# Prompt attention of a hybrid decoder layer: turns of two heads, the compressed branch done once, and GpSimd putting on the weights of both other branches

## The chip, the cores and the metric

The kernel runs on one core of a Trainium2 chip. It is one launch that does a whole inference step of a two-layer trunk. The metric is the device time of that launch in microseconds (us). The engines are TensorE (matmuls; PE in the profile, its weight loads are PEld), VectorE (DVE), ScalarE (ACT), GpSimd (POOL) and SyncE (SP, which issues DMAs). They run their own instruction lists and wait for each other with semaphores that are written out by hand.

## The reference

Two groups of tokens share the weights: one prompt of 256 tokens and 8 decoding sequences of 8 tokens with a past of 1024. Layer 0 mixes with recurrent heads beside twelve attention heads of 64 dimensions; three key/value heads serve four query heads each. An attention head has three branches, and only the prompt's part of it is changed here:

```python
kc = rms_norm(nsa_compress(cmp_all[:, :, 0], ...))      # one key per 32 tokens, every 16
vc = nsa_compress(cmp_all[:, :, 1], ...)
# compressed branch: softmax(q kc^T * scale + bias) vc           (16 columns for the prompt, 15 used)
# selected branch:   softmax(q ks^T * scale + bias) vs           (for 256 tokens every block is selected)
# window branch:     softmax(q kw^T * scale + bias) vw           (window 512 holds the whole prompt)
g = jax.nn.sigmoid(ng).reshape(B, T, NSA_HEADS, 3)
o_n = g[..., 0:1] * o_c + g[..., 1:2] * o_s + g[..., 2:3] * o_w
```

Every branch is causal, has its own softmax and its own gate per token and head.

## The kernel before, in words

All tiles are fp32. Layer 0 runs a feed-forward block, the projections with the recurrent heads woven in, the compress stage, prompt attention, the sample stage (the decoding sequences), an output projection, and the rest.

**Compress stage** (`pe_compress`, `act_compress`, `dve_compress`). The raw cache pages of two sequences at a time are loaded into one of two buffers `raw` (from SP's and POOL's queues, 8 pages each); the load for pair j+2 starts when the products of pair j are done. TensorE multiplies them by `w1c` in six groups g of eight matmuls (L1627). For j=0 the prompt's rows are in the same pass, so the prompt's compressed keys (columns 512 to 527 of `kc`) and values are ready after j=0. DVE adds the halves (`dve_compress_sums`, L1708 and L1712), ACT applies Silu, TensorE makes keys and values (`pe_compress_keys_values`, L1651 and L1656), ACT squares the keys, TensorE sums the squares (`pe_compress_squares`, L1665), ACT takes the root, and DVE normalizes (`dve_compress_keys`). The keys, values and squares of pair j-1 stand in TensorE's list inside the products of pair j; those of the last pair stand in `pe_prompt`.

**Prompt attention** (`pe_prompt`, `act_prompt`, `pool_prompt`, `dve_prompt`). There are 24 turns (c, g, a): c is a pair of heads that share a tile of `proj`, g the half of it (partitions 0 to 63 or 64 to 127), a the half of the prompt's queries; a=0 sees 128 keys, a=1 sees 256. A turn goes TensorE scores of both long branches (L1771, L1772) and of the compressed one (L1777), DVE scale and bias (L1881, L1884) and maxima (L1887, L1888), ACT exponentials with their sums (L1837, three), DVE reciprocals and gates (L1916 to L1921), DVE puts the weights on the window and compressed branch (L1923, L1925), GpSimd on the selected branch (L1865), TensorE transposes (L1823, L1825), ACT and DVE copy them out of PSUM (L1853, L1895), TensorE multiplies by the values (L1800, L1803), ACT copies the result to `mixt` (L1844). The scores are two turns ahead, and `outputs(t-1)` stands behind the transposes of t. `pl` has three slots, the PSUM banks two.

`pe_unread` and `pe_unread_half` are matmuls whose result nobody reads (512 and 256 columns); this document calls them fillers. The sample stage begins with L1965 on TensorE.

The functions that the change touches, with the line numbers of the profile:

Of the kernel before, what the change touches and what calls it, by code (L numbers as in the profile page):

```python
# [24 lines left out]
P = 128  # L25
# [4 lines left out]
TP = 256  # L30
# [170 lines left out]
def build(nc, dram, out):  # L201

    ctx = ExitStack()
    with ctx:
# [81 lines left out]
        vtok = sb([P, 3, C_EVEN])  # L286
        sq2 = sb([P, 2, TOK])
# [47 lines left out]
        ksq = sb([P, 2, NC_COLS])  # L335
# [23 lines left out]
        pl = sb([P, 3, 528])  # L359
        ppt = sb([P, 2, 640])  # L360
        pst = sb([P, 3, 12])
        assert place[0] <= shared + T_Q * TOK
        place[0] = shared + WIN + L_W
# [626 lines left out]
        def dve_setup(dve, chain):  # L990
            setup_loaded.wait(dve, NSETUP)
            dve.wait_ge(toep_done.sem, 1)
            nc.vector.tensor_copy(lines, ps[0:12, 4, 0:384]).then_inc(toep_copied.sem, 1)
            dve.wait_ge(toep_done.sem, 2)
            for a in range(2):
                src = ps[:, 6, 0:384].rearrange("p (n a h) -> p a h n", a=2, h=12)[:, a]
                nc.vector.tensor_tensor(pc_bias[:, a], src, pc_mask[:, a, :].unsqueeze(1).broadcast_to([P, 12, 16]),
                                        ALU.add).then_inc(toep_copied.sem, 1)
# [28 lines left out]

        hsq_ready, hms_ready, hrt_ready, hn_done = (sig(x) for x in ("hsq_ready", "hms_ready", "hrt_ready", "hn_done"))
# [455 lines left out]
        def dve_even(dve, chain):  # L1484
# [34 lines left out]
            toep_ready.wait(dve)  # L1519
# [83 lines left out]
        def pe_compress(pe):  # L1603
# [9 lines left out]
            for j in range(NB // 2):  # L1613
# [46 lines left out]
        def pe_compress_squares(pe, j):  # L1660
            pe.wait_ge(cm_sq.sem, j + 1)
            if j:
                pe.wait_ge(cm_rt.sem, j)
            w = NC_COLS if j == 0 else P
            nc.tensor.matmul(ps[:, 6, 0:2 * w], ones_h[:], ksq[:, :, 0:w], start=True, stop=True).then_inc(cm_ms.sem, 1)  # L1665

        def act_compress(act):
# [13 lines left out]
            for j in range(NB // 2):  # L1681
# [13 lines left out]
                else:  # L1695
                    act.wait_ge(cm_done.sem, j)
                nc.scalar.activation(ksq[:, :, 0:w], keys, ACT.Square).then_inc(cm_sq.sem, 1)
                act.wait_ge(cm_ms.sem, j + 1)
                nc.scalar.activation(ksq[:, :, 0:w], ps[:, 6, 0:2 * w].rearrange("p (a n) -> p a n", a=2), ACT.Sqrt, bias=eps[:])\
                    .then_inc(cm_rt.sem, 1)  # L1700

# [15 lines left out]
        def dve_compress_values(dve, j, chain):  # L1717
            dve.wait_ge(cm_v.sem, j + 1)
            if j == 0:
                chain(nc.vector.tensor_copy(vc[0:16, NB, :], ps[0:16, 7, 0:192]))  # L1720
# [3 lines left out]
        def dve_compress_keys(dve, j, chain):  # L1724
            w = NC_COLS if j == 0 else P
            dve.wait_ge(cm_rt.sem, j + 1)
            chain(nc.vector.reciprocal(ksq[:, :, 0:w], ksq[:, :, 0:w]))
            chain.settle()
            if j == 0:
                chain(nc.vector.scalar_tensor_tensor(kc[:, :, 512:528], kc[:, :, 512:528], small[:, 1:2], ksq[:, :, P:],  # L1730
                                                     ALU.mult, ALU.mult))
            mine = kc[:, :, P * j:P * j + P]
            nc.vector.scalar_tensor_tensor(mine, mine, small[:, 1:2], ksq[:, :, 0:P], ALU.mult, ALU.mult)\
                .then_inc(cm_done.sem, 1)

        def dve_compress(dve, chain):
# [10 lines left out]
            for j in range(NB // 2):  # L1747
                dve_compress_sums(dve, j, chain)
                if j + 1 < NB // 2:
                    dve_compress_values(dve, j, chain)  # L1750
                    dve_compress_keys(dve, j, chain)
# [3 lines left out]
        TURNS = [(c, g, a) for c in range(6) for g in range(2) for a in range(2)]  # L1755
        gates_ready = sig("gates_ready")
        pa_sc, pa_lg, pa_ex, pa_rg, pa_p, pa_tr, pa_pt, pa_ptc, pa_o, pa_oc = (
            sig("prompt_" + x) for x in ("scores", "logits", "exps", "gated_sums", "weights", "turned", "turned_copied",
                                         "turned_copied_c", "outputs", "outputs_copied"))

        def pe_prompt(pe):
            pe.wait_ge(cm_done.sem, 1)
            pe.wait_ge(cm_sum.sem, NB // 2 - 1)

            def token_scores(t):
                c, g, a = TURNS[t]
                s, r, x, nk = t % 2, slice(64 * g, 64 * g + 64), int(c >= 4), P * (a + 1)
                q = proj[r, T_Q + c, P * a:P * a + P]
                if t >= 2:
                    pe.wait_ge(pa_lg.sem, t - 1)  # L1770
                nc.tensor.matmul(ps[:, s, 0:nk], q, proj[r, T_KS + x, 0:nk], start=True, stop=True)  # L1771
                nc.tensor.matmul(ps[:, s, 256:256 + nk], q, proj[r, T_KW + x, 0:nk], start=True, stop=True)  # L1772

            def block_scores(t):
                c, g, a = TURNS[t]
                r = slice(64 * g, 64 * g + 64)
                nc.tensor.matmul(ps[:, 2 + t % 2, 0:16], proj[r, T_Q + c, P * a:P * a + P], kc[r, int(c >= 4), 512:528],  # L1777
                                 start=True, stop=True).then_inc(pa_sc.sem, 1)

            def scores(t):  # L1780
                token_scores(t)
                block_scores(t)
            token_scores(0)
            token_scores(1)
            pe_unread(7, 2)
            pe.wait_ge(cm_sum.sem, NB // 2)
            block_scores(0)
            block_scores(1)
            pe_compress_keys_values(pe, NB // 2 - 1)

            def outputs(t):
                c, g, a = TURNS[t]
                s, kv = t % 2, HEADS[2 * c + g] // 4
                pe.wait_ge(pa_pt.sem, t + 1)
                pe.wait_ge(pa_ptc.sem, t + 1)
                r = slice(64 * g, 64 * g + 64)
                first_ = True
                for br, cv in ((0, C_VS), (1, C_VW)):
                    for k in range(a + 1):
                        nc.tensor.matmul(ps[r, 6 + s, 0:P], vtok[:, k, cv + HD * kv:cv + HD * kv + HD],  # L1800
                                         ppt[:, s, P * (2 * br + k):P * (2 * br + k) + P], start=first_, stop=False)
                        first_ = False
                nc.tensor.matmul(ps[r, 6 + s, 0:P], vc[0:16, NB, HD * kv:HD * kv + HD], ppt[0:16, s, 512:640],  # L1803
                                 start=False, stop=True).then_inc(pa_o.sem, 1)

            pe_unread(7, 2)
            pe_compress_squares(pe, NB // 2 - 1)
            for t, (c, g, a) in enumerate(TURNS):
                s = t % 2
                if t + 2 < len(TURNS):  # L1810
                    scores(t + 2)
                if t >= 2:
                    pe.wait_ge(pa_pt.sem, t - 1)
                    pe.wait_ge(pa_oc.sem, t - 1)
                elif t == 0:
                    pe_unread(7, 3)
                    pe.wait_ge(cm_vc.sem, NB // 2)
                    pe.wait_ge(cm_rt.sem, NB // 2)
                pe_unread_half(4 + s)
                pe.wait_ge(pa_p.sem, t + 1)  # L1820
                for br in range(2):
                    for k in range(a + 1):
                        nc.tensor.transpose(ps[:, 4 + s, P * (2 * br + k):P * (2 * br + k) + P],  # L1823
                                            pl[:, t % 3, 256 * br + P * k:256 * br + P * k + P], ident[:])
# [1044 lines left out]
```

## Time and profile before

| | us |
|---|---|
| median of 3 runs (lowest, highest) | 1846.71 (1843.71, 1846.82) |
| the profiled execution's own time | 1845.96 |
| its span, first to last instruction | 1844.2 |

Over the span TensorE is busy 1748.0 us (95%), DVE 1055.7 (57%), ACT 560.4 (30%) and GpSimd 154.3 (8%). The mean granted clock of TensorE is 0.966 of full speed. A busy TensorE is not TensorE at its peak: matmuls are pipelined, and one record's duration overlaps the next. An fp32 matmul leaves two records, each with a weight load; a transpose leaves one. The share of 1.00 is 2.4 GHz and 0.50 is 1.2 GHz.

### The profile page before, as it was taken

What the parts mean: (1) busy time and instruction counts of PE and PEld (TensorE: products, weight loads), DVE (VectorE), ACT (ScalarE), POOL (GpSimd) and SP (SyncE); (2) the same over time, 40 slices, a digit from 0 to 9 for tenths busy, and PEclk for the clock granted to TensorE, in tenths of its full rate; (3) what the DMA queues carried; (4) which work ended last, traced back from release to release, by engine and by line L of the source; (5) the groups of instructions that cost most, each with busy time, mean ns of one, the idle gap of its engine ahead of it and who ended that gap; (6) DMA issues with size and microseconds to landing.
All of it is one profiled execution on the core that took longest, in us unless ns stands there. A gap on an engine that the chain in (4) does not pass through costs nothing.

```text
span 1844.2 us, 28453 instructions
## 1 busy us (share of the span) xinstructions
PE 1748.0 (95%) x11424; PEld 1502.9 (81%) x11424; DVE 1055.7 (57%) x1521; ACT 560.4 (30%) x812; POOL 154.3 (8%) x155
## 2 busy tenths in 40 slices
PE   6999999999999989999999999999999767999998
PEld 6999986777886754579999979999977535999996
DVE  6776633445745744347776547776515735777642
ACT  5333320012224623224343224343201313434321
POOL 1000020000120213110000101110100001000010
PEclk9999998999899989999999999999999788999999
DMA  4435454222460405346665326666334451444432
GB/s 182 149 146 192 157 179 151 71 78 98 137 224 1 155 1 175 141 148 250 249 250 210 108 105 235 229 258 263 139 136 171 173 214 68 153 142 162 157 108 74
DMA packets 48815, 287.82 MB, mean 156 GB/s; under 512 B 7492, under 2 KB 18400, under 8 KB 24640
## 3 DMA queue, kind: packets, MB, share of 16 engines
q1 hardware_dynamic: 43184, 236.26, 35.3%
q0 software_dynamic: 5552, 50.46, 7.6%
q8 instruction: 54, 0.88, 0.2%
q14 instruction: 25, 0.20, 0.0%
HBM read 280.51 MB, written 41.62 MB: 175 GB/s over the span
## 4 chain that ended last, share of the span: by engine, by line
PE 83%; DVE 9%; ACT 3%; DMA 2%; issue 2%; SPq 0%; POOL 0%; POOLq 0%; DVEq 0%; ACTq 0%
PE ps L698 15%; PE ps L699 15%; PE ps L700 15%; PE ps L710 6%; PE ps L1372 6%; PE ps L1425 3%; PE ps L2289 2%; DVE w_lo L689 2%; ACT w_hi L683 2%; PE ps L1627 2%; PE ps L1296 2%; DVE mem L677 1%; PE ps L1800 1%; PE ps L896 1%; PE ps L2033 1%
## 5 line engine op out<-in xcount | busy, mean ns | idle before, releaser
L698 PE MATMUL ps<-x_hi,w_hi 128*128 128x320 f32 x1408 | 438.6, 312 | 29.0 <-DVE w_lo L689 22.3
L699 PE MATMUL ps<-x_lo,w_hi 128*128 128x320 f32 x1408 | 437.2, 310 | 0.0
L700 PE MATMUL ps<-x_hi,w_lo 128*128 128x320 f32 x1408 | 437.1, 310 | 0.0
L689 DVE TENSOR_TENSOR w_lo<-live,w_hi 128x2048 fp32r<-128x2048 f32 (+1 forms) x120 | 300.6, 2505 | 180.7 <-ACT w_hi L683 180.7
L683 ACT ACTIVATE w_hi<-mem 128x2048 fp32r<-128x2048 f32 (+1 forms) x120 | 250.3, 2086 | 257.7 <-DVE mem L677 257.7
L698 PEld LDWEIGHTS ps<-x_hi,w_hi 128*128 128x128 f32 x1408 | 266.1, 189 | 33.7 <-DVE w_lo L689 25.5
L699 PEld LDWEIGHTS ps<-x_lo,w_hi 128*128 128x128 f32 x1408 | 266.4, 189 | 0.0
L700 PEld LDWEIGHTS ps<-x_hi,w_lo 128*128 128x128 f32 x1408 | 266.2, 189 | 0.0
L698 PE MATMUL ps<-act_hi,w_hi 128*128 128x320 f32 x704 | 218.4, 310 | 7.0 <-DVE w_lo L689 7.0
L700 PE MATMUL ps<-act_hi,w_lo 128*128 128x320 f32 x704 | 217.5, 309 | 0.0
L699 PE MATMUL ps<-act_lo,w_hi 128*128 128x320 f32 x704 | 217.5, 309 | 0.0
L677 DVE TENSOR_SCALAR mem<-live 128x2048 int32<-128x2048 int32 (+1 forms) x120 | 161.1, 1342 | 5.8 <-DMA live<-in_w_fi 3.4
L698 PEld LDWEIGHTS ps<-act_hi,w_hi 128*128 128x128 f32 x704 | 132.1, 188 | 9.1 <-DVE w_lo L689 9.1
L551 POOL TENSOR_TENSOR mem<-mem 128x640 f32<-128x640 f32 x24 | 58.7, 2445 | 937.9 <-ACT mem L545 937.9
L699 PEld LDWEIGHTS ps<-act_lo,w_hi 128*128 128x128 f32 x704 | 132.1, 188 | 0.0
L700 PEld LDWEIGHTS ps<-act_hi,w_lo 128*128 128x128 f32 x704 | 132.1, 188 | 0.0
L800 ACT ACTIVATE mem<-mem 128x320 f32<-128x320 f32 x88 | 41.6, 473 | 295.0 <-DVE mem L835 294.9
L1372 PE MATMUL ps<-live 128*128 128x320 f32 x400 | 118.4, 452 | 4.8 <-DVE mem L1007 2.9
L710 PE MATMUL ps<-live 128*128 128x320 f32 x448 | 122.2, 432 | 0.0
L710 PEld LDWEIGHTS ps<-live 128*128 128x128 f32 x448 | 85.0, 190 | 35.0
L1372 PEld LDWEIGHTS ps<-live 128*128 128x128 f32 x400 | 77.0, 197 | 37.7 <-issue 6.7
L835 DVE TENSOR_TENSOR mem<-ps,live 128x320 f32<-128x320 f32 x88 | 43.2, 491 | 56.7 <-PE ps L700 56.6
(392 smaller groups left out, 2041.8 us busy)
## 6 DMA issues: line engine op xcount, KB each, us to landing
live<-in_w_fi SPq DMA_DIRECT2D x88, 1024.0 KB, 4.8
live<-in_w_fo SPq DMA_DIRECT2D x32, 1408.0 KB, 6.2
mem<-in_dil SPq DMA_DIRECT2D x16, 1152.0 KB, 11.0
out_old_dil<-in_old_dil POOLq DMA_DIRECT2D x8, 2032.0 KB, 9.0
live<-in_w_even SPq DMA_DIRECT2D x12, 1024.0 KB, 4.9
live<-in_w_gate SPq DMA_DIRECT2D x8, 1024.0 KB, 4.8
out_old_dil<-in_old_dil POOLq DMA_DIRECT2D x8, 1008.0 KB, 7.4
mem<-in_slc SPq DMA_DIRECT2D x32, 192.0 KB, 4.0
```

The source lines that it names most:

```text
L551: nc.gpsimd.tensor_tensor(sq_sum[:], sq_sum[:], sq_new[:], ALU.add).then_inc(sq_summed.sem, 1)
L677: nc.vector.tensor_scalar(w_masked[:, slot, 0:w].bitcast(I32), ring[:, slot, 0:w].bitcast(I32), HI_BITS, None, ALU.bitwise_and).then_inc(w ...
L683: nc.scalar.activation(w_hi[:, slot, 0:w], w_masked[:, slot, 0:w], ACT.Copy).then_inc(w_hi_ready.sem, 1)
L689: nc.vector.tensor_tensor(w_lo[:, slot, 0:w], ring[:, slot, 0:w], w_hi[:, slot, 0:w].bitcast(F32), ALU.subtract).then_inc(w_split.sem, 1)
L698: nc.tensor.matmul(out, wh, hi, start=first_k, stop=False)
L699: nc.tensor.matmul(out, wh, lo, start=False, stop=False)
L700: return nc.tensor.matmul(out, wl, hi, start=False, stop=last_k)
L710: last = nc.tensor.matmul(ps[:, 2 * slot + a, 0:TOK], w[:, a, k, :], xn[:, k, :], start=(k == 0), stop=(k == DT - 1))
L800: nc.scalar.activation(silu_t[:, 1 - s, 0:TOK], silu_t[:, 1 - s, 0:TOK], ACT.Silu)\
L835: nc.vector.tensor_tensor(b[:, 0:TOK], ps[:, 2 * (1 - s), 0:TOK], rstds[0], ALU.mult)\
L1372: last = nc.tensor.matmul(ps[:, 2 * slot + a, 0:TOK], ring[:, slot, c:c + P], xn[:, k, :], start=(k == 0), stop=(k == DT - 1))
L1425: last = nc.tensor.matmul(ps[:, 2 * slot, TP * tt:TP * tt + TP], xn[:, k, tt * P:tt * P + P], ring[:, slot, k * TP:(k + 1) * TP], start=(k ...
```

## The change

- A turn is now (c, a): both heads of a tile, so 12 turns. TensorE's scores and outputs alternate the two heads, matmul by matmul.
- The compressed branch of all heads and queries is done once, inside the compress stage: scores after group 0 of pair 2, one softmax over 24 x 16 columns with the gates multiplied in, 24 matmuls that turn the weights (12 after group 0 and 12 after group 4 of pair 3), two copies. Its values are copied three times to partitions 0, 32 and 64, and each turn starts its outputs with that branch.
- GpSimd puts on the weights of both long branches (four instructions per turn); DVE only makes them.
- `pe_compress_squares(j-1)` stands before the products of group 5 instead of behind them; `ksq` has two slots; ACT's wait for the normalized keys is for the pair before last.
- Scores, logits and exponentials of turn 0 stand inside the compress stage.
- `ppt` moves to the space of `xn`. The setup of `pc_bias` orders the heads by half, in eight instructions instead of two.

The diff's core; the functions of prompt attention printed above are replaced as a whole, so only new lines stand here. Signals, reshapes and places in memory are left out.

```diff
 # pe_compress, in the loop over g
+                    if j and g == 5:
+                        pe_compress_squares(pe, j - 1)
                     (products of group g)
-                    elif g == 5:
-                        pe_compress_squares(pe, j - 1)
+                    if (j, g) == (2, 0):
+                        pe_block_scores(pe)
+                    elif (j, g) in ((3, 0), (3, 4)):
+                        pe_block_turned(pe, g // 4)
+                    elif (j, g) == (3, 1):
+                        pe.wait_ge(cm_sum.sem, 3)
+                        pe_prompt_scores(pe, 0)
 # pe_compress_squares
+            if j == 1:
+                pe.wait_ge(pb_dve.sem, B_LOGITS)
 # act_compress, behind the squares of pair j, and behind its root
+                if j == 1:
+                    act.wait_ge(pb_dve.sem, B_LOGITS)
+                    nc.scalar.activation(pcf, pcf, ACT.Exp).then_inc(pb_act.sem, 1)
...
+                if j == 2:
+                    act_prompt_exps(act, 0)
 # dve_compress
+            dve_compress_sums(dve, 1, chain)
+            dve_block_logits(dve, chain)
+            dve_compress_values(dve, 1, chain)
+            dve_block_weights(dve, chain)
+            dve_compress_keys(dve, 1, chain)
+            dve_compress_sums(dve, 2, chain)
+            dve_block_copy(dve, 0)
+            toep_ready.wait(dve)
+            dve_prompt_logits(dve, 0, chain)
+            dve_compress_values(dve, 2, chain)
+            dve_block_copy(dve, 1)
+            dve_compress_sums(dve, 3, chain)
+        def pe_block_scores(pe):
+            pe.wait_ge(cm_done.sem, 1)
+            pe.wait_ge(cm_vc.sem, 1)
+            pe.wait_ge(cm_rt.sem, 1)
+            for c, a in TURNS:
+                for g in range(2):
+                    r, at_ = head_rows(g), 16 * (6 * a + c)
+                    last = nc.tensor.matmul(ps[:, 7 - g, at_:at_ + 16], proj[r, T_Q + c, P * a:P * a + P],
+                                            kc[r, int(c >= 4), 512:528], start=True, stop=True)
+            last.then_inc(pb_pe.sem, 1)
+        def pe_block_turned(pe, half):
+            pe.wait_ge(pb_dve.sem, B_WEIGHTS + half)
+            for u in range(12 * half, 12 * half + 12):
+                b, at_ = 32 * (u % 3), P * (u // 3 % 4)
+                last = nc.tensor.matmul(ps[b:b + 16, 7, at_:at_ + P], pcf[:, 16 * u:16 * u + 16], ident[:],
+                                        start=True, stop=True, tile_position=(0, b))
+            last.then_inc(pb_pe.sem, 1)
+        def pe_prompt_scores(pe, t):
+            c, a = TURNS[t]
+            x, nk = int(c >= 4), P * (a + 1)
+            if t >= 2:
+                pe.wait_ge(pa_lg.sem, t - 1)
+            for br, keys in ((0, T_KS + x), (1, T_KW + x)):
+                for g in range(2):
+                    r = head_rows(g)
+                    last = nc.tensor.matmul(ps[:, 2 * (t % 2) + g, TP * br:TP * br + nk], proj[r, T_Q + c, P * a:P * a + P],
+                                            proj[r, keys, 0:nk], start=True, stop=True)
+            last.then_inc(pa_sc.sem, 1)
+        def pe_prompt(pe):
+            pe.wait_ge(cm_sum.sem, NB // 2)
+            pe_prompt_scores(pe, 1)
+            pe.wait_ge(pb_dve.sem, B_COPIED + 1)
+            pe_unread(7, 4)
+            pe_compress_keys_values(pe, NB // 2 - 1)
+            pe_unread(7, 2)
+            pe_compress_squares(pe, NB // 2 - 1)
+            def outputs(t):
+                c, a = TURNS[t]
+                bank = 7 - t % 2
+                pe.wait_ge(pa_pt.sem, 2 * t + 2)
...
+                for g in range(2):
...
+                    nc.tensor.matmul(ps[head_rows(g), bank, 0:P], vcp[b:b + 16, v:v + HD], ptb[b:b + 16, u // 3, :],
+                                     start=True, stop=False, tile_position=(b, 64 * g), skip_group_check=True)
+                for br, cv in ((0, C_VS), (1, C_VW)):
+                    for k in range(a + 1):
+                        for g in range(2):
...
+                            last = nc.tensor.matmul(ps[head_rows(g), bank, 0:P], vtok[:, k, v:v + HD],
...
+                last.then_inc(pa_o.sem, 1)
+            for t, (c, a) in enumerate(TURNS):
+                if t + 2 < len(TURNS):
+                    pe_prompt_scores(pe, t + 2)
+                for g in range(2):
+                    if t:
+                        pe.wait_ge(pa_pt.sem, 2 * t - 1 + g)
+                    elif g:
+                        pe.wait_ge(cm_vc.sem, NB // 2)
+                    pe_unread_half(4 + g)
+                    pe.wait_ge(pa_p.sem, 2 * t + g + 1)
+                    (2 (a + 1) transposes of head g).then_inc(pa_tr.sem, 1)
+                if t:
+                    outputs(t - 1)
+            outputs(len(TURNS) - 1)
+        def act_prompt(act):
+            for t, (c, a) in enumerate(TURNS):
+                if t + 1 < len(TURNS):
+                    act_prompt_exps(act, t + 1)
+                (for each head g: wait for pa_tr 2 t + g + 1, copy its transposes, pa_pt)
+                if t:
+                    out_copy(t - 1)
+            out_copy(len(TURNS) - 1)
+        def pool_prompt(pool):
+            for t, (c, a) in enumerate(TURNS):
+                s, nk = (t + 2) % 3, P * (a + 1)
+                pool.wait_ge(pa_rg.sem, t + 1)
+                for g in range(2):
+                    for br in range(2):
+                        v, i = pl[:, s, g, TP * br:TP * br + nk], 8 + 2 * g + br
+                        last = nc.gpsimd.tensor_scalar(v, v, pst[:, s, i:i + 1], None, ALU.mult)
+                    last.then_inc(pa_p.sem, 1)
+        def dve_prompt(dve, chain):
+            weights(0)
+            dve_prompt_logits(dve, 1, chain)
+            dve_compress_keys(dve, NB // 2 - 2, chain)
+            dve_compress_values(dve, NB // 2 - 1, chain)
+            for t in range(1, len(TURNS)):
+                if t + 1 < len(TURNS):
+                    dve_prompt_logits(dve, t + 1, chain)
+                weights(t)
+                if t in (2, 3):
+                    last_keys(t - 2)
```

`dve_prompt_logits` does one scale-and-bias instruction for each head and one maximum over the four rows of columns; `weights(t)` is one reciprocal and one multiply by the gates. `act_prompt_exps` does four exponentials.

## Rows read from the trace of the kernel before

**Rows 1.** Windows: stretch, its us, busy us of each engine, PEclk, DMA share, GB/s

```profile
567.00:584.00 17.00, 14.90 (x57) 8.50 (x56) 8.41 (x22) 8.80 (x20) 0.01 (x1) 0.80 0.00 1
616.00:632.00 16.00, 16.00 (x104) 12.32 (x103) 11.65 (x55) 9.91 (x41) 3.67 (x6) 1.00 0.76 250
1443.00:1480.00 37.00, 30.19 (x139) 23.57 (x140) 24.25 (x50) 12.86 (x32) 0.00 (x0) 0.69 0.14 57
```

**Rows 2.** Chain that ended last, 561 to 664 us: start, us, what

```profile
561.56 0.58 PE ps L1651 x8
562.14 0.69 PE ps L1656 x12
...
566.60 0.45 PE ps L1665 x2
...
569.89 0.96 DVE mem L1708
...
571.91 1.13 ACT mem L1687 x2
...
580.48 1.28 ACT L1837
...
627.68 0.44 PE ps L1823 x4
...
634.08 0.44 PE ps L1823 x4
...
662.18 1.51 PE ps L1965 x16
```

**Rows 3.** Timeline of PEld, 553 to 555 us: start, us, [idle before <-releaser]

```profile
554.14 0.97 PEld L1627 LDWEIGHTS ps<-mem 128*128 128x128 f32 x8 [0.55 <-DMA mem<-in_cmp]
```

**Rows 4.** Timeline of PE, 628 to 631 us, part of a head

```profile
628.15 0.65 PE L1800 MATMUL ps<-mem 128*64 128x128 f32 x4
628.73 0.43 PE L1803 MATMUL ps<-mem 16*64 16x128 f32 x2
629.09 0.48 PE L1771 MATMUL ps<-mem 64*128 64x128 f32 x2
...
629.64 0.29 PE L1777 MATMUL ps<-mem 64*128 64x16 f32 x2
629.86 0.70 PE L1601 MATMUL ps<-live 128*128 128x256 f32 x2
630.40 0.38 PE L1823 MATMUL ps<-live,mem 128*128 128x128 f32 x2
630.62 0.27 PE L1825 MATMUL ps<-live,mem 128*16 128x128 f32 x1
630.82 1.09 PE L1800 MATMUL ps<-mem 128*64 128x128 f32 x8
```

**Rows 5.** Timeline of PE in three earlier and later places, small matmuls alternating

```profile
340.30 0.71 PE L1293 MATMUL ps<-mem 64*128 64x128 f32 x8
...
443.67 1.97 PE L1421 MATMUL ps<-live 128*64 128x128 f32 x32
...
699.02 1.19 PE L2033 MATMUL ps<-mem 128*32 128x64 f32 x39
```

**Rows 6.** Groups by shape, 567 to 662 us: busy us, mean ns | idle before

```profile
L1837 ACT ACTIVATE mem<-mem 128x256 f32<-128x256 f32 x24 | 11.9, 498 | 0.1
L1865 POOL TENSOR_SCALAR mem<-mem 128x256 f32<-128x256 f32 x12 | 11.1, 922 | 20.2 <-DVE mem L1925 20.2
...
L1881 DVE SCALAR_TENSOR_TENSOR mem<-ps,live 128x512 f32<-128x512 f32 x12 | 8.3, 690 | 15.3 <-PE ps L1777 15.3
L1887 DVE TENSOR_REDUCE mem<-mem 128x2 f32<-128x512 f32 x12 | 8.2, 686 | 0.4
...
L1865 POOL TENSOR_SCALAR mem<-mem 128x128 f32<-128x128 f32 x12 | 7.2, 602 | 69.4 <-DVE mem L1925 69.4
...
L1920 DVE TENSOR_TENSOR mem<-mem 128x2 f32<-128x2 f32 x24 | 3.9, 161 | 0.8
```

More of the change, by code:

```diff
@@ L286, in build @@
         vtok = sb([P, 3, C_EVEN])
+        norms_at = place[0]
         sq2 = sb([P, 2, TOK])
@@ L1746, in dve_compress @@
             chain.settle()
[L1747 to L1751, printed above, removed]
+            dve_compress_sums(dve, 0, chain)
+            dve_compress_values(dve, 0, chain)
+            dve_compress_keys(dve, 0, chain)
+            dve_compress_sums(dve, 1, chain)
+            dve_block_logits(dve, chain)
+            dve_compress_values(dve, 1, chain)
@@ L1756, in build @@
         gates_ready = sig("gates_ready")
-        pa_sc, pa_lg, pa_ex, pa_rg, pa_p, pa_tr, pa_pt, pa_ptc, pa_o, pa_oc = (
+        pa_sc, pa_lg, pa_ex, pa_rg, pa_p, pa_tr, pa_pt, pa_o, pa_oc = (
             sig("prompt_" + x) for x in ("scores", "logits", "exps", "gated_sums", "weights", "turned", "turned_copied",
-                                         "turned_copied_c", "outputs", "outputs_copied"))
-        def pe_prompt(pe):
[L1762 to L1784, printed above, removed]
@@ new lines, in dve_block_weights @@
+        def dve_block_weights(dve, chain):
+            gates_ready.wait(dve)
+            for a in range(2):
+                v = vtok[:, a, C_NG:C_NG + 36].rearrange("p (h c) -> p h c", c=3)[:, :, 0]
+                chain(nc.vector.tensor_scalar(v, v, pc_some[:, a:a + 1], None, ALU.mult))
+            dve.wait_ge(pb_act.sem, 1)
+            chain(nc.vector.tensor_reduce(bst[:, 1], pc3, AX.X, ALU.add))
+            chain.settle()
+            chain(nc.vector.reciprocal(bst[:, 1], bst[:, 1]))
+            chain.settle()
+            w = bst[:, 1].rearrange("p (a h) -> p a h", a=2)
+            gates = vtok[:, 0:2, C_NG:C_NG + 36].rearrange("p a (h c) -> p a h c", c=3)[:, :, :, 0]
+            for at_, heads in BY_HALF:
+                n = len(range(12)[heads])
+                chain(nc.vector.tensor_tensor(w[:, :, at_:at_ + n], w[:, :, at_:at_ + n], gates[:, :, heads], ALU.mult))
+            chain.settle()
+            nc.vector.tensor_tensor(pc3, pc3, bst[:, 1].unsqueeze(2).broadcast_to([P, 24, 16]), ALU.mult).then_inc(pb_dve.sem, 1)
@@ L1798, in outputs @@
                 for br, cv in ((0, C_VS), (1, C_VW)):
                     for k in range(a + 1):
[L1800 to L1809, printed above, removed]
-                if t + 2 < len(TURNS):
[L1811 to L1824, printed above, removed]
-                nc.tensor.transpose(ps[0:16, 6 + s, P:2 * P], pl[:, t % 3, 512:528], ident[:]).then_inc(pa_tr.sem, 1)
+                        for g in range(2):
+                            v = cv + HD * (HEADS[2 * c + g] // 4)
+                            last = nc.tensor.matmul(ps[head_rows(g), bank, 0:P], vtok[:, k, v:v + HD],
+                                                    ppt[:, t % 2, g, P * (2 * br + k):P * (2 * br + k) + P],
+                                                    start=False, stop=(br == 1 and k == a), skip_group_check=True)
```

203 lines of the change are left out of this document (105 added, 98 removed).

## The prediction

> **What bounds the kernel now.** I read the stage table of the stretch first, then the chain that ended last inside it, then TensorE's instructions of one head, then the groups by shape. In the steady part of prompt attention TensorE is busy for all of 16 us at the full clock, and GpSimd for 3.67 [rows 1]. The chain shows the same place in the loop 6.40 us apart, from 627.68 to 634.08 [rows 2]: one head (a turn with a=0 and one with a=1) costs 6.40 us, two heads 12.80, and nearly all of it is TensorE. The compress stage before it ends with the squares of the third page group at 567.05 (566.60 + 0.45), and the sample stage begins at 662.18 [rows 2], so the last compress work and prompt attention together take 95.1 us. In their first 17 us the granted clock averages 0.80 [rows 1]: TensorE waits there for a serial chain. The reader should see two costs: a slow start, and a loop that pays TensorE by the instruction.
>
> **What a head's instructions cost TensorE.** From start to start [rows 4]: the two score matmuls of an a=0 turn 0.55 (629.09 to 629.64), the compressed scores 0.22, the filler 0.54, two transposes 0.22, the small transpose of compressed weights 0.20, the output matmuls 0.58 for two and about 1.0 for four (1.09 with the last drain), the compressed output 0.36.
>
> **Removed from the loop.** Compressed scores and small transposes: (0.22 + 0.20) x 4 turns per two heads = 1.7 us of 12.80. DVE and ACT lose their compressed instructions too, and DVE its multiply of one branch; these lie beside TensorE and only free queues.
>
> **Paired on TensorE.** The new order alternates the two heads, which sit in the two row halves (scores) and the two column halves (outputs). The trace has both patterns elsewhere. Eight records alternating in row halves, 128 columns, take 0.71 us [rows 5], where the loop's eight would take about 1.0; 32 records in alternating column halves take 1.97, so a pair of records shares one slot of 0.11 (16 slots, and the last drain). So I price a turn's scores at 0.7 (a=0) and, with twice the columns, 1.1 (a=1); outputs of both heads at 0.36 + 0.58 = 0.95 (a=0) and 0.36 + 1.0 = 1.4 (a=1). Two fillers per turn stay (0.54, and 0.45 as an estimate where no other tile shape precedes), and four or eight transposes (0.44 or 0.88). An a=0 turn, which runs the outputs of an a=1 turn, is 0.7 + 1.0 + 0.44 + 1.4 = 3.5; an a=1 turn 1.1 + 1.0 + 0.88 + 0.95 = 3.9. TensorE alone would need 7.4 us for two heads.
>
> **What the loop then waits for.** All weights of both branches go to GpSimd: four instructions per turn, 0.602 each for 128 keys and 0.922 for 256 [rows 6], so 2.4 or 3.7 us between gates and transposes, where before there was one. GpSimd's own sum is 6.1 per two turns and ACT's exponentials are eight of at most 0.50; neither is the bound. The chain through them is: scores of turn t+1 with their drain 0.9, their logits on DVE, the weights of turn t behind them in DVE's queue 0.4 (two tiny instructions of 0.16 [rows 6] and a settle), 0.1 to GpSimd, its four instructions, 0.5 for the last transposes, the outputs of t-1, and then the scores of t+2 may start. For a=1 in t, logits (a=0) are two instructions of an estimated 0.4 (0.69 for 512 elements) and a reduction over 512 of 0.69 [rows 6], 1.5 in all: 0.9 + 1.5 + 0.4 + 0.1 + 3.7 + 0.5 + 0.95 = 8.05 us per two turns. For a=0 in t, logits (a=1) are two of 0.69 less overlap and a reduction over 1024, estimated at 1.2, so 2.5: 1.2 + 2.5 + 0.4 + 0.1 + 2.4 + 0.3 + 1.4 = 8.3, but the first half of the four instructions suffices for the first transposes and TensorE does a filler in between, which takes 0.4 off. I take 8.05, above TensorE's 7.4. Bounds per two heads: 7.4 (GpSimd's fixed part, 0.28 per instruction by the two rows, hidden behind its predecessor) and 10.4 (nothing pairs: 3.0 more on TensorE).
>
> On where this work belongs the Trainium skill speaks against the change: GPSIMD Engine Reference, Engine selection, gives elementwise work to VectorE, though it puts one-input operations on GpSimd at roughly line rate. No row here agrees with line rate (0.922 us for 256 elements); by it the loop would run at TensorE's 7.4, which is the second rival.
>
> **Added to the compress stage.** TensorE is its bound, so every matmul counts.
> - 24 compressed scores after the first group of the third page pair: in pairs 12 x 0.22 + 0.4 for two changes of shape = 3.0; unpaired 5.3. Against it stands the 0.55 that TensorE waited for pages just afterwards [rows 3]: +2.45.
> - 24 matmuls that turn the weights, in three column groups: 39 records of 64 columns took 1.19 [rows 5], 13 sets; twice the columns and 16 sets give about 2.6; unpaired 5.2.
> - the scores of turn 0: 0.7.
>
> The compress stage ends at 567.05 + 5.75 = 572.8. DVE's softmax of the compressed branch (some eight instructions, estimated at 4 us in all), the three copies of values and ACT's Exp with two table loads of 1.28 [rows 2] run under the page products. Walked through in order they end about when TensorE comes to its waits (the tightest is the sums of the third page pair, before turn 0's scores); if one is late, TensorE stands by that much, with the last page products behind it. I cost them at nothing; bound 5 us. DVE's six more small instructions at the setup lie under projections: nothing.
>
> **From there to the loop.** Sums of the last page pair 2.1 (569.89 to 571.91, and the signal), in which TensorE idles; scores of turn 1 1.1; six full fillers, 0.9 each (an estimate: twice the columns of the 0.54, without its change of shape), 5.4; keys and values 0.58 + 0.69 = 1.3; squares 0.45 [rows 2]: 10.35, so 583.15. Logits, exponentials and weights of turn 0 are then long done, which in before stood in the path (the Exp table load is on the chain at 580.48).
>
> **The loop and its end.** Turn 1's exponentials stand behind the last roots and a table load on ACT: 0.6 + 1.3 + 2.0 before the weights, where steady turns have 2.4: the first two turns take 9.5. Five more pairs 5 x 8.05 = 40.25; the last keys on DVE 1.0; copies and outputs of the last turn 1.9. Sum 52.65: the sample stage begins at 635.8 instead of 662.18, 26.4 earlier.
>
> **Clock.** Two gaps remain: 2.1 us before turn 1's scores, and in turn 1 some 4 us of waiting in pieces. In before such a start cost the clock: it averaged 0.80 over 17 us [rows 1]. I take 2.5 us for each (bounds 0 and 6), 5 in all. Gain 26.4 - 5 = 21.4. The profiled execution took 1845.96 us (span 1844.2), 0.75 under the median of 1846.71, so **1824.6 against its own time, 1825 against the median**.
>
> The Trainium skill, TensorE: Matmul & The Clock Gate, Why this matters for your kernels, says that idle gaps between bursts of matmuls bring the clock back to half. That is the third rival's mechanism. The trace agrees in the odd layer's prompt loop: from 1443 to 1480 TensorE was busy 30.2 of 37 us and the granted clock averaged 0.69 [rows 1].
>
> **Rivals.**
> 1. Forecast: paced by GpSimd's chain, with a late wait in the compress stage up to 5 us possible: 1819 to 1831. Chance 0.57.
> 2. GpSimd's fixed part hides and the clock holds: 7.4 per pair saves 0.65 x 5.5 = 3.6, and no 5 for the clock: gain 30, 1816. Against it: every instruction in before stood alone, so nothing shows overlap. 0.13.
> 3. The gate bites in the loop as in the odd layer, whose mean of 0.69 is 62% of the time at half. At half TensorE needs 14.8 per pair: the pace becomes 1/(0.62/14.8 + 0.38/8.05) = 11.2, 3.2 x 5.5 = 17.4 more than at full: gain 9, 1837. For it: pairing leaves TensorE waiting 0.65 of 8.05. Against it: the fillers stay, and at half clock TensorE has no gaps. 0.16.
> 4. The pairing does not occur in the loop's order: 10.4 per pair, 14 more, and 5 more in compress: gain 7.5, 1838. Against it rows 5. 0.07.
> 5. Slower than before: the loop stays at half clock throughout, 14.8 per pair, 6.75 x 5.5 = 37 more, and 2.5 at the start: 1859. It decides against the change from a pace of 12.85, which is 82% of the loop at half. The odd layer's row is nearest; that the steady loop of before holds 1.00 speaks against. 0.05. Another 0.02 is no change.
>
> **How the numbers follow.** The likeliest is the forecast, 1825, with its own range of 1819 to 1831. To hold 8 in 10 the range takes in rival 2 and rival 3: 1816 to 1838. A difference of about 0.2% is what the times of this kernel can tell from none. Faster by more: 0.57 + 0.13 + 0.16 + 0.07 = 0.93, less a little for several small losses together, 0.91; same 0.03; slower 0.06.
>
> **What would show it.** The chain of the loop should repeat per two turns in about 8 us, with GpSimd's multiply between DVE and TensorE on it and TensorE waiting for it; scores and outputs should start in pairs a few ns apart. The compress stage should end near 573 and the first transposes come near 585. The granted clock should dip once or twice between 573 and 595 and then be 1.00. The prediction is wrong if TensorE is without gaps in the loop (rival 2 at 7.4 or rival 4 at 10.4), if the clock of the loop averages under 0.9 (rival 3), or if TensorE waits in the compress stage for DVE's softmax.

## The result, and the profile after

The changed kernel took 1823.97 us (median of 4 runs, 1821.44 to 1826.82) beside 1845.26 for the kernel before (4 runs): a ratio of 0.9885, 95% interval 0.9864 to 0.9906. The profiled execution took 1825.9, its span is 1824.2, 20.0 shorter than that of before.

The chain of waits of the changed kernel first. It answers to [rows 2]; columns as there.

```profile
545.34 2.78 PE ps L1811 x48
...
560.94 0.99 PE ps L1848 x24
...
563.91 0.65 PE ps L1865 x8
...
571.58 0.99 PE ps L1848 x24
...
573.20 1.80 PE ps L1638 x16
...
585.02 0.45 PE ps L1683 x2
...
610.00 1.09 PE ps L1865 x8
...
611.11 1.30 DVE mem L1969 x2
...
612.43 1.22 DVE mem L1974
613.65 0.09 DVE mem L1984
...
613.77 0.17 DVE mem L1987
...
614.03 2.36 POOL mem L1958 x4
...
616.43 0.44 PE ps L1913 x2
616.87 0.36 PE ps L1890 x4
617.24 1.02 PE ps L1896 x16
618.26 1.09 PE ps L1865 x8
...
640.41 1.54 PE ps L2045 x16
```

The first five rows are what the compress stage was given and its last products, which end at 575.00. The middle is one turn of the loop's wheel, from 610.00 to 618.26: scores of an odd turn, their logits on DVE (L1969, L1974), the weights of the even turn that stand behind them (L1984, L1987), GpSimd's four multiplies, the transposes and the outputs of the turn before. It repeats every 8.26 us, where [rows 2] has 12.80 for two heads.

Windows of the changed kernel (columns as in [rows 1]): the start of the loop, then a full period.

```profile
585.00:593.00 8.00, 5.45 (x35) 3.38 (x33) 4.95 (x11) 6.47 (x21) 3.14 (x4) 1.00 0.00 0
593.00:602.00 9.00, 8.45 (x56) 5.90 (x58) 3.63 (x9) 3.85 (x15) 5.96 (x9) 0.62 0.07 17
...
614.03:622.29 8.26, 7.92 (x70) 5.41 (x72) 4.54 (x10) 5.89 (x23) 5.98 (x8) 1.00 0.73 209
```

The granted clock fell to half once (a dip, from 594.0 to 600.8), after the waits of the second turn (TensorE busy 5.45 of 8 us), and was 1.00 from 602 to the end of the loop. No engine is busy for the whole of the steady period; the chain of waits fills it.

To compare stages I count from the first output matmul of the recurrent heads inside the compress stage (L1350 before, L1360 after), since it came 2.4 us later in this profile (515.36 for 512.94) and 2.1 earlier in a second profile of the same kernel (e10). From there to the sample stage:

| us | before | forecast | after | after, second profile |
|---|---|---|---|---|
| to the end of the compress stage | 54.1 | 59.9 | 59.6 | 59.8 |
| to the last squares (bridge) | | 10.35 | 10.5 | 12.0 |
| to the sample stage (loop and end) | | 52.65 | 54.9 | 55.1 |
| clock | in the rows | 5.0 | in the rows | in the rows |
| sum | 149.2 | 127.9 | 125.1 | 127.0 |

Of the 24.2 us that the stage gained, 2.4 were lost ahead of it, where among other things TensorE waited 4.54 us for a load of weights (`in_w_even`) instead of 1.92, and 1.7 behind it, where the clock was at half for 83 us instead of 80 (from the sample stage to the end 1183.8 for 1182.1). The second profile has 1183.5 behind the stage with 80 us at half, so the clock is not the whole of that.

### The profile page after: what moved, and what is told of

The parts are those of the page before. It is cut to its first block, busy times and chain, and to the rows that moved or that the text cites. A ratio compares the mean times of both kernels' runs of the same rounds, so it can differ in the third digit from the quotient of the medians.

```text
span 1824.2 us, 28222 instructions
## 1 busy us (share of the span) xinstructions
PE 1720.4 (94%) x11446; PEld 1476.6 (81%) x11446; DVE 1035.1 (57%) x1362; ACT 551.8 (30%) x755; POOL 171.9 (9%) x179
## 4 chain that ended last, share of the span: by engine, by line
PE 82%; DVE 9%; ACT 3%; DMA 3%; issue 1%; POOL 1%; POOLq 0%; SPq 0%; DVEq 0%; ACTq 0%
PE ps L704 15%; PE ps L706 15%; PE ps L705 15%; PE ps L716 6%; PE ps L1382 6%; PE ps L1435 3%; PE ps L1638 3%; PE ps L2369 2%; DVE w_lo L695 2%; ACT w_hi L689 2%; PE ps L1306 2%; DVE mem L683 1%; DMA live<-in_w_fo 1%; PE ps L2113 1%; DMA live<-in_w_even 1%
```

## The experiments

The first four ran together on one chip, the next four together, the last three together. Whole launches of one kernel scatter by 5 to 24 us here, in part because dips of the clock fall now in one stage and now in another. So the stage (the sum in the table above) and the pace, read from each run's profile, carry the verdicts, and the ratios stand beside them. Each run has one profile, and its stage has dips of its own; the last column is half of the time that the stage spent at half clock, which is the most that the dips can have cost it. For before it is 3.4.

| kernel | median us | ratio to before, interval | stage us | pace, us per two heads | dips in the stage, at most us |
|---|---|---|---|---|---|
| changed | 1823.97 | 0.9885, 0.9864 to 0.9906 | 125.1 | 8.26 | 3.4 |
| e1, weights first | 1833.32 | 0.9907, 0.9873 to 0.9941 | 130.6 | 8.5 to 8.7 | 8.2 |
| e2, no multiplies | 1816.73 | 0.983, 0.9748 to 0.9911 | 118.5 | 7.49 | 3.4 |
| e3, unpaired | 1837.67 | 0.9922, 0.988 to 0.9963 | 140.3 | 9.79 | 8.5 |
| e4, window on DVE | 1815.87 | 0.9803, 0.973 to 0.9876 | 119.1 | 7.49 | 1.7 |
| e5, no fillers | 1834.56 | 0.9917, 0.9879 to 0.9955 | 130.2 | 9.68 mean | 13.7 |
| e6, e4 and an earlier start | 1817.01 | 0.9818, 0.9735 to 0.9901 | 118.4 | 7.49 | 3.4 |
| e7, e4, no fillers | 1827.51 | 0.9872, 0.978 to 0.9965 | 124.1 | 8.64 mean | 13.7 |
| e8, squares behind | 1829.71 | 0.9879, 0.9792 to 0.9966 | 127.3 | 8.26 | 5.1 |
| e9, e6, one filler | 1820.41 | 0.9815, 0.9769 to 0.986 | 117.0 | 7.21 | 3.4 |
| e10, changed again | 1825.27 | 0.9841, 0.979 to 0.9892 | 127.0 | 8.25 | 5.1 |
| e11, e4 again | 1820.79 | 0.9811, 0.9761 to 0.986 | 119.3 | 7.49 | 1.7 |

The means of e5 and e7 take in the end of the loop, a last period without scores; without it they are 9.35 and 8.52.

**e1: the order of DVE's queue.**

```diff
+                weights(t)
                 if t + 1 < len(TURNS):
                     dve_prompt_logits(dve, t + 1, chain)
-                weights(t)
```

> DVE makes the weights of turn t before the logits of turn t+1, where the changed kernel has them the other way round. After the change the chain of the loop repeats every 8.26 us: scores of an odd turn 1.09, its logits on DVE 2.56, the weights of the even turn 0.28, GpSimd's four multiplies of 128 columns 2.36, transposes 0.44, outputs 1.38. Theory A, it is the order of DVE's queue that puts the 2.56 in the chain: the pace falls to TensorE's own need, about 7.6 us, and the launch gets 3 us shorter, to about 1821. Theory B, the order only passes the wait on: DVE now waits for the exponentials of turn t before it makes the logits of t+1, ACT has its exponentials of t+1 before the copies of t, and TensorE waits for those: a pace of 8.0 to 8.3 and 0 to 2 us more.

Theory B, and more than its 8.0 to 8.3: the pace rose to 8.47 and 8.69. The stage rose to 130.6, but by less than 1 us when the dips are taken off (122.4 for 121.7 and 121.8 of the two profiles of the changed kernel). Its chain of waits no longer touches TensorE or GpSimd:

```profile
605.31 0.77 DVE mem L1969 x2
...
606.10 0.70 DVE mem L1974
606.82 1.25 ACT mem L1928 x6
...
608.29 0.20 ACT mem L1928
608.51 0.19 DVE mem L1984
608.72 0.04 DVE mem L1987
...
608.80 1.30 DVE mem L1969 x2
```

DVE waits for the exponentials (L1928) of the turn whose logits it has just made, and only then makes the next ones: logits, exponentials and weights now run one after the other. The swap took one link out of the chain and put another in.

**e2 and e4: what GpSimd's multiplies cost.** In e2 GpSimd multiplies one column per head, so the weights are left off:

```diff
-                    for br in range(2):
-                        v, i = pl[:, s, g, TP * br:TP * br + nk], 8 + 2 * g + br
-                        last = nc.gpsimd.tensor_scalar(v, v, pst[:, s, i:i + 1], None, ALU.mult)
-                    last.then_inc(pa_p.sem, 1)
+                    v, i = pl[:, s, g, 0:1], 8 + 2 * g
+                    nc.gpsimd.tensor_scalar(v, v, pst[:, s, i:i + 1], None, ALU.mult).then_inc(pa_p.sem, 1)
```

> GpSimd multiplies one column per head instead of four blocks per turn, so the weights are not put on and the outputs are not normalized. It prices GpSimd in the loop. Theory A (GpSimd's 2.36 us for an even turn are a link of the chain, TensorE is close behind): the pace falls from 8.26 to TensorE's own need, 7.1 to 7.6 us, TensorE shows no gaps, and the launch gets 4 to 6 us shorter (1818 to 1820). Theory B (TensorE is the bound and its gaps are only drawn so): no change of pace. Theory C (GpSimd alone is the bound): the pace falls by more than 2.4 us, to under 5.9, and the launch by 13 us or more.

In e4 GpSimd keeps the selected branch and DVE takes the window branch, behind its weights (the transposes wait for both):

```diff
 # pool_prompt: one multiply for each head, of 0:nk
 # dve_prompt, end of weights(t)
+                dve.wait_ge(pa_rg.sem, t + 1)
+                for g in range(2):
+                    v, i = pl[:, s, g, TP:TP + P * (a + 1)], 8 + 2 * g + 1
+                    nc.vector.tensor_scalar(v, v, pst[:, s, i:i + 1], None, ALU.mult).then_inc(pa_pw.sem, 1)
```

> DVE puts on the weights of the window branch, as it did before the change, and GpSimd those of the selected branch alone; turns of two heads and the compressed branch stay as changed. Theory A (GpSimd is a link of the chain): GpSimd's link of an even turn halves from 2.36 to 1.2 us, DVE's two multiplies run beside it, and the pace falls from 8.26 to about 7.2 to 7.6, where TensorE bounds it; the launch gets 4 to 6 us shorter (about 1819). Theory B (taking the work off DVE is where the change gains): DVE's logits come later by its four multiplies per two turns, about 1.2 us, and the launch gets 3 to 7 us longer.

Theory A in both. Windows of one period, e2 and then e4:

```profile
601.86:609.35 7.49, 7.49 (x70) 5.57 (x72) 4.54 (x10) 5.78 (x23) 1.07 (x4) 1.00 0.77 226
```

```profile
605.63:613.12 7.49, 7.49 (x70) 5.57 (x72) 5.97 (x15) 5.78 (x22) 3.25 (x4) 1.00 0.82 261
```

Both are TensorE's own need, 7.49 us without a gap. So for the pace, half of the multiplies on DVE is as good as none at all: DVE had room (4.54 us of 8.26) and pays 1.4 for them. e4 and the changed kernel ran once more beside each other:

> The changed kernel as it is, beside the others on one chip: 0.9885 of the kernel before if the chip makes no difference, a loop of 8.26 us per two heads, and 125 us from the first output of the recurrent heads inside the compress stage to the sample stage.

> Window weights on DVE once more, beside the changed kernel on one chip. If GpSimd's link of the loop is what it costs, 6 us less than the changed kernel (0.985 of the kernel before), and 7.49 us per two heads.

The stage is 6.0 us shorter in the first pair of profiles and 7.6 in the second (119.07 for 125.06, 119.32 for 126.95). With the dips taken off it is 4.3 and 4.2, so 1.7 and 3.4 us of the two differences are dips that were absent, which this edit is not shown to bring: behind the stage both profiles of e4 take longer (1187.1 and 1187.2 us, for 1183.8 and 1183.5), with 7 to 14 us more at half clock. The medians differ by 4.5, but the runs overlap, so that e4 beats the changed kernel is shown in the stage, not by the launches' intervals.

**e3: heads one after the other.**

```diff
-            for br, keys in ((0, T_KS + x), (1, T_KW + x)):
-                for g in range(2):
+            for g in range(2):
+                for br, keys in ((0, T_KS + x), (1, T_KW + x)):
 # and likewise all outputs of head 0 ahead of those of head 1
```

> The scores and the outputs of a turn go head after head instead of alternating; nothing else differs. Theory A (matmuls in different row or column halves share time): the odd turn's scores grow from 1.09 to about 2.0 and the outputs of four blocks from 1.38 to about 2.3, the pace from 8.26 to about 10 us, and the launch gets 9 to 11 us longer (about 1834). Theory B (the order of the two heads makes no difference, and the gain is that of the compressed branch): 0.

Theory A, with a surprise. Its chain of waits:

```profile
611.14 0.65 PE ps L1865 x8
...
613.29 0.36 PE ps L1890 x2
613.65 1.02 PE ps L1895 x8
614.67 0.36 PE ps L1890 x2
615.02 1.02 PE ps L1895 x8
616.04 1.07 PE ps L1865 x8
```

The outputs doubled (1.38 to 2.76 for an odd turn, 0.95 to 1.88 for an even one), in all 2.3 us: TensorE's need goes from 7.49 to 9.79, and it now sets the pace. The scores (L1865) did not move: 0.65 and 1.07, as when alternating. The stage takes 13 to 15 us more than the changed kernel's, 10 of them with the dips taken off.

**e5, e7 and e9: the fillers and the clock.** e5 is the changed kernel, e7 is e4, both with `pe_unread_half(4 + g)` taken out of the loop.

> The changed kernel without the two fillers per turn; nothing else differs. With GpSimd out of the loop TensorE needed 7.49 us per two heads, of which the four fillers are 2.1. Theory A (the chain through DVE and GpSimd sets the pace and the fillers lie in its waits): the pace stays 8.26, TensorE is busy for 5.4 of it, the clock stays at 1.00 and the launch within 2 us of the changed kernel's 1824. Theory B (the fillers hold the clock): TensorE has gaps of a third of the loop, and the granted clock falls as in the odd layer (mean 0.69, 62% of the time at half). At half TensorE needs 10.7, the mean pace is 1/(0.62/10.7 + 0.38/8.26) = 9.6, and the launch 7 us longer, about 1831.

> Window weights on DVE and no fillers in the loop. TensorE needs 7.49 - 2.1 = 5.4 us per two heads. Walked through the queues, the loop then hangs on scores, logits, exponentials, copies and outputs at about 6.9, ACT being busy 5.8 of it and DVE 6.0. Theory A (the clock holds): a pace of 6.9 and a launch 3 us shorter than with fillers, about 1813. Theory B (gaps of a fifth to a quarter of the loop cost the clock): at half TensorE needs 10.8, the mean pace with 62% of the time at half is 1/(0.62/10.8 + 0.38/6.9) = 8.9, and the launch is 8 us longer, about 1824.

Theory B in both. Windows of four successive periods of e5, the last of them the end of the loop:

```profile
601.64:610.91 9.27, 7.33 (x62) 5.11 (x64) 4.54 (x10) 5.92 (x23) 6.38 (x10) 0.84 0.72 235
610.91:620.01 9.10, 6.86 (x62) 4.72 (x62) 4.54 (x10) 6.00 (x22) 6.73 (x10) 0.90 0.80 249
620.01:629.69 9.68, 7.25 (x62) 4.98 (x62) 4.45 (x10) 6.04 (x23) 5.68 (x8) 0.85 0.74 241
629.69:640.35 10.66, 7.96 (x53) 5.22 (x54) 3.10 (x7) 6.03 (x23) 6.83 (x10) 0.66 0.11 34
```

and two of e7:

```profile
608.18:616.34 8.16, 7.53 (x62) 5.30 (x64) 5.84 (x14) 5.80 (x23) 2.02 (x3) 0.80 0.79 243
616.34:624.88 8.54, 7.22 (x62) 4.98 (x62) 5.83 (x15) 5.79 (x22) 4.51 (x6) 0.82 0.78 255
```

With less to do TensorE takes longer: the granted clock is never 1.00 over a period, and dips cost the stage of either up to 13.7 us, for 3.4 and 5.1 in the changed kernel and 1.7 in e4. e9 leaves out one filler of two (that ahead of the second head's transposes) from e6, which follows below.

> The kernel with window weights on DVE and the second turn started earlier, with one of the two fillers of each turn left out (that ahead of the second head's transposes). TensorE needs 7.49 - 0.87 = 6.6 us per two heads and the chain through DVE, ACT and the copies 6.9, so TensorE would be busy 95% of the loop. Theory A (small gaps leave the clock alone): a pace of 6.9 at a clock of 1.00 and 3 us less than with both fillers, about 1813. Theory B (any regular gap costs it, as with no fillers): dips to half in the loop, where the pace is 13.2, a mean over 7.5, and 0 to 8 us more than with both fillers, 1816 to 1824.

```profile
615.17:622.38 7.21, 7.02 (x66) 4.80 (x68) 5.79 (x15) 5.67 (x22) 3.27 (x4) 1.00 0.83 255
```

Theory A for the clock: the profile shows TensorE idle for 0.19 us per period, and the clock at 1.00. The pace is 7.21 and not 6.9, since the second head's transposes then wait: in an even turn they start 0.63 us behind the first head's, which need 0.22. The stage is 117.0, 1.4 less than e6. The launch's own interval can't tell the two.

**e6: an earlier start.**

```diff
 # act_compress, ahead of the copies of the last keys
+                if j == NB // 2 - 1:
+                    act_prompt_exps(act, 1)
 # act_prompt
-                if t + 1 < len(TURNS):
+                if t and t + 1 < len(TURNS):
 # dve_prompt: for t == 1, weights(t) ahead of dve_prompt_logits(t + 1)
```

> Window weights on DVE as in the run before, and the second turn started earlier: its exponentials stand ahead of ACT's copies of the last keys (so ahead of the last square root and its two table loads), and its weights on DVE ahead of the logits of the third turn. In the run with the window weights on DVE the last squares ended at 582.0, then came root 0.5, table load 1.28, exponentials 2.1, weights 0.4, multiplies 0.9, and the second turn's transposes at 588.5. Theory A (that chain sets the start): the transposes come at about 583.5 and the launch gets 4 to 5 us shorter, about 1811. Theory B (the work is only moved: the last root with its two table loads now holds back the exponentials of the third turn): the third turn comes later by what the second gains, 0 to 1 us.

Theory A in kind, not in size. From the end of the compress stage to the sample stage it takes 57.1 us for e4's 59.0: 1.9 instead of 4 to 5. TensorE's rows show why:

```profile
583.78 0.38 PE L1917 MATMUL ps<-live,mem 128*128 128x128 f32 x2
...
586.34 0.60 PE L1917 MATMUL ps<-live,mem 128*128 128x128 f32 x4
```

The second turn's transposes come at 586.34, 15.8 us after the end of the compress stage, where e4 has them 17.7 after it (587.53). The 588.5 of the expectation were the second head's. There is no wait between the fillers of the last keys and them: the two turns' scores, fillers and transposes fill TensorE. The expectation had forgotten its own work.

**e8: the squares.** The squares of pair j-1 stand behind the products of group 5 again, as before the change.

> The changed kernel with the squares of page pair j-1 behind the products of group 5 again, as before the change. Theory A (the move only spares a wait that other work covers): the root of the second pair comes 2 us later, its keys on DVE stand ahead of the third pair's sums, and these end about 5.4 us after the products, just when TensorE reaches its wait for them; 0 to 1 us, 1824 to 1825. Theory B (the move was needed): TensorE stands at that wait for up to 3 us and the clock drops after it, 3 to 6 us, 1827 to 1830.

Neither theory as it stands: there is a wait, but at another place than either named. TensorE's rows:

```profile
546.80 3.78 PE L1811 MATMUL ps<-mem 64*128 64x16 f32 x48 [1.26 <-DVE mem L1758]
550.52 7.91 PE L1636 MATMUL ps<-live,mem 128*128 128x128 f32 x48
```

The new block scores (L1811) wait 1.26 us for the normalized keys of the first pair, which come later with later squares; then the clock is at half for the scores (3.78 for 2.85) and the products behind them (7.91 for 5.62). The compress stage ends 4.2 to 4.4 us later than in the two profiles of the changed kernel, counted as in the table. Only the wait can be put down to the order of the squares. The same dip came in four runs that keep the squares where the change put them (e2, e3, e6 and e9, 3.4 to 6.8 us at half), and in e6 and e9 TensorE had not waited just ahead of it; so whether the wait brought the dip in e8 is not shown. In e3 it is as deep as here, and the compress stage ends 63.2 us after its start, for 64.0 in e8:

```profile
542.57 3.19 PE L1811 MATMUL ps<-mem 64*128 64x16 f32 x48
545.69 8.50 PE L1638 MATMUL ps<-live,mem 128*128 128x128 f32 x48
```

The whole stage of e8 is 0.3 to 2.2 us longer than the changed kernel's, and about 0.4 with the dips taken off, the size that theory A gave. The medians of the launches (1829.71 for 1823.97 and 1825.27) look like theory B, but their intervals overlap.

## Why the prediction was right, point by point

**The compress stage.** Forecast +5.75, measured +5.5. The parts erred both ways: block scores 2.78 (3.0), the turned weights 1.98 (2.6), turn 0's scores 0.65 (0.7), together 0.9 less; what I did not price is the cutting of the products into more groups, to which the other 0.6 go. Such a cut costs about 0.1 at some places and nothing at others: 16 products take 1.98 behind keys and values or turned weights, 1.80 behind squares, and 1.85 on the mean in a run of 48. DVE's softmax of the compressed branch was hidden, as assumed: TensorE waits in the stage for nothing in both profiles of the changed kernel. That holds only with the squares moved, an edit that I had costed at nothing; e8 shows that it spares a wait of 1.26. It was also luck that neither profile has the dip behind the block scores: e2, e3, e6 and e9 have it, and there the stage grew by 7 to 9.

**The bridge.** 10.35 forecast, 10.5 measured, in one profile without a dip. In the second the gap of 2.1 us (TensorE waits for the sums) was followed by half clock: the fillers took 5.40 us instead of 3.70.

**The pace.** 8.05 forecast, 8.26 measured. I had written down two chains, one through each kind of turn, and took the 8.05 of the first. The chip takes the second one, the even turn's weights behind the odd turn's logits, and its terms were close: 1.2, 2.5, 0.4, 0.1, 2.4, 0.3 and 1.4 forecast, 1.09, 2.56, 0.28, 0.08, 2.36, 0.44 and 1.38 measured. The step that failed is the 0.4 taken off because half of the multiplies suffices for the first transposes: the second head's transposes wait for the last multiply, so all four count. Without it the sum is 8.3. The first chain, by the rows measured since, adds up to about 7.5 (an estimate: scores 0.65, logits 0.77 and 0.70, weights 0.28 and 0.08, multiplies 3.63, transposes 0.44, outputs 0.95) and is not on the path, so that its 8.05 came near 8.26 is luck.

**TensorE's need.** 7.4 forecast, 7.49 measured (e2, e4). The unpaired bound, 3.0 more, whose working the prediction does not show, was 2.3 (e3), because scores pair in either order. Of the 5.3 us by which the need fell from 12.80, e3 shows these 2.3 for the outputs. The scores went from 3.0 (twice 0.55 and 0.97) to 1.7, and the 1.7 that are left are what the prediction gave to the compressed branch; no run puts either of them back alone, so this part of the split is argued.

**The clock.** Two gaps at 2.5 each. One profile shows only the second (0.62 of full over 9 us, 6.8 us at half: up to 3.4 lost), the other both (1.7 lost on the fillers, and again 6.8 us at half, 0.88 and 0.73 over the two windows: up to 5.1 in all), for 5.

**Start and end of the loop.** 54.94 less four periods of 8.26 is 21.9, dip included; forecast 52.65 less four of 8.05, 20.45, without a dip. Without its dip it is about 18.5: some 2 too much in my forecast, which made up for the pace. So the total, 1825 beside 1823.97, is better than its terms: each of compress stage, pace, clock and ends was off by 0.2 to 2 us, and they cancelled in part. What was left, a stage 2.8 us shorter than forecast in the first profile, went with the 4.1 lost ahead of it and behind it, which the forecast does not have.

**The rivals.** Rival 2 needed GpSimd's fixed part to hide behind the multiply before. It does not: four in a row take 2.36 or 3.63 us, 0.59 or 0.91 each, against 0.602 and 0.922 alone [rows 6]. The Trainium skill, GPSIMD Engine Reference, Engine selection, gives such elementwise work to VectorE, and the rows agree: alone, DVE needs 0.29 or 0.35 us (last section) for what costs GpSimd 0.60 or 0.92. Its remark that one-input work is roughly at line rate on GpSimd is not borne out: 128 further columns cost GpSimd 0.32 us and DVE 0.07. Rival 3 is real, but the fillers keep it away: e5 lands on its mechanism, a mean pace of 9.68, in a kernel that differs by them alone. Rival 4 fell with e3, which costs 1.5 us of pace and 13 to 15 of the stage (10 without the dips). Two side sums are off without changing a choice: rival 4's 14 us are 12.9 by its own pace (2.35 times 5.5), and the dividing pace of 12.85 in rival 5 leaves out its 2.5 us at the start, with which it is 12.4.

**Where the gain went.** The change as a whole saves 22 to 24 us of the stage, but one of its parts takes some back: with the window branch left on DVE the same kernel saves 30 (28 for 24 with the dips taken off). Whether the compressed branch done once pays by itself no run shows.

## What to carry to other kernels

An engine with 8% of the span busy can still sit on the chain: count a moved instruction at its full length in the loop's longest dependency, not in its engine's total, and split the work so that both engines do it side by side. Pair small matmuls of different column halves by alternating them in the list. Matmuls without a reader in a loop that waits are not waste: take them away one at a time, and look at the granted clock of each period. Where dips of the clock come and go from run to run, take them off a stage before its length is put down to an edit: e8 is an example.

## What the runs showed of the hardware

**Row halves paired in both orders, column halves only in alternation.** Eight score records of 256 columns take 1.07 to 1.09 us in either order of the heads (e3; they start in pairs, 13 ns apart in e3 and 7 in the changed kernel), where one head's four took 0.97 in the loop of before (0.54 and 0.43 from start to start). Output records in column halves, in e3 with all six or ten of a head ahead of the other's, took the full double. In e3 a head's four score records stand together, and its six or ten output records, so whether the kind of half or this distance decides is not shown.

**GpSimd and DVE slow each other when both multiply.** First DVE's multiply of the window branch in the kernel before, where GpSimd never multiplies at the same time (the view of [rows 6]), then GpSimd's multiplies with DVE making logits and maxima beside them (the changed kernel):

```profile
L1923 DVE TENSOR_SCALAR mem<-mem 128x256 f32<-128x256 f32 x12 | 4.2, 353 | 0.4
L1923 DVE TENSOR_SCALAR mem<-mem 128x128 f32<-128x128 f32 x12 | 3.4, 287 | 0.4
```

```profile
L1958 POOL TENSOR_SCALAR mem<-mem 128x256 f32<-128x256 f32 x13 | 11.8, 924 | 1.1 <-DVE mem L1987 1.1
L1958 POOL TENSOR_SCALAR mem<-mem 128x128 f32<-128x128 f32 x12 | 7.0, 605 | 6.9 <-DVE mem L1987 6.9
```

Then the four multiplies of one turn of e4 in the order of their starts (608.31, 608.37, 608.58 and 609.44 us): DVE's first, GpSimd's first, DVE's second, GpSimd's second. The same view is taken over four windows that hold one of them each.

```profile
L1992 DVE TENSOR_SCALAR mem<-mem 128x256 f32<-128x256 f32 x1 | 0.4, 355 | 0.0
L1959 POOL TENSOR_SCALAR mem<-mem 128x256 f32<-128x256 f32 x1 | 1.1, 1082 | 1.4 <-DVE mem L1987 1.4
L1992 DVE TENSOR_SCALAR mem<-mem 128x256 f32<-128x256 f32 x1 | 0.6, 569 | 0.0
L1959 POOL TENSOR_SCALAR mem<-mem 128x256 f32<-128x256 f32 x1 | 0.9, 917 | 0.0
```

Beside logits and maxima a GpSimd multiply is as long as alone (924 and 605 ns, 922 and 602 in [rows 6]). In e4 GpSimd's first multiply, with DVE's beside it, takes 1082 ns (695 for 128 columns), and its second, with none beside it, 917 (597). DVE's first, which starts ahead of GpSimd's, keeps its 355 (288), and its second, which stands beside GpSimd's first from end to end, takes 569 (395). The Trainium skill, SBUF — State Buffer, Who interferes with whom, names this: such a multiply on DVE can take the pair of memory ports that it shares with GpSimd, a reduction never does, and the second to ask waits for the whole instruction. The trace agrees on which operations collide, and not on the wait: GpSimd's first grows by 160 ns where it runs beside DVE's first for 295, and DVE's second ends at 609.15, while GpSimd's first runs to 609.45.
